# Model rows numbered in blocks of 128, the last token tile of each mixer turned and scored in column halves, its norm root on GpSimd, and fewer unread transposes

## What is computed

```python
for i in range(DEPTH):
    hn = rms_norm(h, norm_mix[i])
    h = h + (mla_mixer if i % 2 == 0 else gla_mixer)(hn, ...)
    h = h + hier_moe(rms_norm(h, norm_ffn[i]), ...)
return h[:, N_META:N_META + S]

def rms_norm(x, g):
    return x * rsqrt(mean(x * x, axis=-1) + EPS) * g

def hier_moe(t, ...):                       # 32 experts, D_EXPERT = 256
    g_logits = t @ w_rg + b_rg              # 4 groups: argmax
    e_logits = t @ w_re + b_re              # 8 experts of that group: top 2
    for e in range(N_EXPERTS):
        hid = silu(t @ w_gate[e]) * (t @ w_up[e])
        out = out + gates[:, e:e + 1] * (hid @ w_down[e])
```

## Time and profile before

| | us |
|---|---|
| median of 3 runs | 722.73 (720.85 to 727.63) |
| profiled execution, its time | 727.45 |
| span of that execution | 725.7 |
| PE busy | 653.9 (90%) |
| DVE busy | 245.9 (34%) |
| ACT busy | 149.1 (21%) |
| POOL busy | 41.2 (6%) |

### The profile page before, as it was taken

The page is one execution under the profiler, slowest core; times in us unless marked ns, Lnnn a source line. Parts: engine busy times, 40 slices in busy tenths (PEclk is TensorE's granted clock), DMA queues, the critical chain, the costliest instruction groups (busy, mean ns, idle before and its releaser), DMA issues.

```text
span 725.7 us, 11565 instructions
## 1 busy us (share of the span) xinstructions
PE 653.9 (90%) x5148; PEld 389.1 (54%) x5148; DVE 245.9 (34%) x522; ACT 149.1 (21%) x293; POOL 41.2 (6%) x62
## 2 busy tenths in 40 slices
PE   7999899999999977999789999989999996687686
PEld 6654775467456535635358644564665552434332
DVE  2136874154332331333053811321533331123112
ACT  2135663631001100000023412123310110000000
POOL 2033110000000000000020600010000000000000
PEclk9999999999999997999999999999999998899899
DMA  8910553737999999999993505644879999999995
GB/s 349 379 53 1 231 234 145 320 144 305 428 438 428 429 426 428 432 429 424 431 431 163 202 29 233 261 203 186 336 315 433 433 429 431 414 440 430 420 425 238
DMA packets 12311, 234.09 MB, mean 323 GB/s; under 512 B 1552, under 2 KB 1872, under 8 KB 3168
## 3 DMA queue, kind: packets, MB, share of 16 engines
q1 hardware_dynamic: 11936, 233.09, 76.5%
q10 hardware_dynamic: 320, 0.18, 0.1%
HBM read 232.22 MB, written 1.05 MB: 321 GB/s over the span
## 4 chain that ended last, share of the span: by engine, by line
PE 69%; DMA 25%; issue 2%; DVE 2%; ACT 1%; SPq 0%; DVEq 0%; ACTq 0%
DMA mem<-in_experts 23%; PE ps L945 10%; PE ps L1112 8%; PE ps L670 7%; PE ps L967 7%; PE ps L921 7%; PE ps L959 5%; PE ps L790 4%; PE ps L1103 4%; PE ps L742 3%; PE ps L732 1%; DMA mem<-in_mla_w_in 1%; PE ps L715 1%; PE ps L810 1%; PE ps L686 1%
## 5 line engine op out<-in xcount | busy, mean ns | idle before, releaser
L945 PE MATMUL ps<-mem,hT 128*32 128x256 f32 x1952 | 120.3, 393 | 25.7 <-DMA mem<-in_experts 25.6
L945 PEld LDWEIGHTS ps<-mem,hT 128*32 128x32 f32 x1952 | 65.0, 113 | 81.5 <-DMA mem<-in_experts 33.1
L921 PE MATMUL ps<-mem,rows 128*128 128x128 f32 x560 | 71.4, 290 | 16.1 <-issue 16.1
L921 PEld LDWEIGHTS ps<-mem,rows 128*128 128x128 f32 x560 | 68.7, 204 | 22.1 <-issue 22.1
L967 PE MATMUL ps<-hT,mem 128*128 128x512 f32 x160 | 76.4, 609 | 2.1 <-DVE hT L1788 1.8
L1794 DVE TENSOR_TENSOR rows<-rows,ps 128x512 f32<-128x512 f32 (+1 forms) x80 | 54.2, 684 | 59.2 <-PE ps L967 59.1
L959 PE MATMUL ps<-mem 128*32 128x512 f32 x496 | 59.1, 606 | 7.7 <-DMA mem<-in_experts 5.4
L670 PE MATMUL ps<-mem,hT 128*128 128x512 f32 x128 | 57.1, 598 | 2.9 <-ACT hT L1428 2.9
L1112 PE MATMUL ps<-mem,hT 128*128 128x512 f32 x128 | 55.6, 594 | 0.0
L1348 ACT ACTIVATE mem<-ps 128x256 f32<-128x256 f32 x16 | 9.9, 620 | 218.2 <-PE ps L945 218.2
L967 PEld LDWEIGHTS ps<-hT,mem 128*128 128x128 f32 x160 | 24.0, 170 | 49.5 <-issue 49.5
(11 more groups left out here) (303 smaller groups left out, 674.5 us busy)
## 6 DMA issues: line engine op xcount, KB each, us to landing
mem<-in_experts SPq DMA_DIRECT2D x34, 4096.0 KB, 31.9
mem<-in_experts SPq DMA_DIRECT2D x24, 2048.0 KB, 17.4
mem<-in_gla_parts SPq DMA_DIRECT2D x4, 4096.0 KB, 25.4
rows<-in_experts SPq DMA_DIRECT2D x4, 2048.0 KB, 34.4
mem<-in_mla_o SPq DMA_DIRECT2D x1, 4096.0 KB, 30.3
mem<-in_mla_w_in SPq DMA_DIRECT2D x2, 1344.0 KB, 10.2
mem<-in_mla_uq SPq DMA_DIRECT2D x1, 2304.0 KB, 16.9
mem<-in_mla_ukv SPq DMA_DIRECT2D x1, 2048.0 KB, 23.5
```

Of the source, the lines that this page charges most:

```text
L921: mm = pe.matmul(ps[:, k // 4, (k % 4) * P:(k % 4 + 1) * P], xn[:, i, k, :], Sg[:, i, :], start=i == 0, stop=i == nt - 1)
L945: mm = pe.matmul(ps[32 * j:32 * j + 32, 2, m * FE:(m + 1) * FE], xe[:, k, 32 * j:32 * j + 32], w[:, j, c * FE:(c + 1) * FE], start=k == 0 ...
```

## The change

The numbering of model rows changes from stride 8 to blocks of 128 (piece k holds rows 128k to 128k+127), in the kernel's views and in the host's layout of all weights. With it a half of the columns of a tile holds four whole pieces, and tile 1 is turned, multiplied by its gain, and scored in two halves; its first half is turned ahead of `ranks(early)`, right behind the last product. The scores stand ahead of all of `gathered(early)`. On DVE `gained(n, 1)` moves ahead of `ranked` and `sent`. The squares of the expert norms stay on ACT (those of tile 1 in two halves, each after its add), the roots go to GpSimd. `BUSY` goes from 24 and 36 to 6 and 14, `FILL` is gone. ACT gets an `Exp` of one element behind `scaled(1)`.

```diff
-    FILL, BUSY = [3, 5], [24, 36]
+    BUSY = [6, 14]
+    HALVED = (1, 3)
+    HT0 = [sum(NORM_TILES[:i]) + sum(m < i for m in HALVED) for i in range(5)]
 # gpsimd, ahead of its wait for moe_done, and again at its end with n = 3
+        def roots(n):
+            for i in ORDER[n]:
+                pool.wait_ge(ffn_squared, rstd_count(n, i))
+                v = ssq[:, i:i + 1]
+                link(pool.tensor_scalar(v, v, ssq_right if i == 1 else 0.0, EPS, ALU.add, ALU.add))
+                pool.tensor_tensor(rstd[:, i:i + 1], v, half_root[:, i:i + 1], ALU.pow).then_inc(rstd_ok, 1)
 # tensor
-        def turn(i, src):
-            for k in range(KD):
+        def turn(i, ks=range(KD)):
+            for k in ks:
...
-                mm = pe.transpose(dst, src[0:R, k, :], ident[0:R, 0:R])
+                mm = pe.transpose(dst, h[i][0:R, k * P:(k + 1) * P], ident[0:R, 0:R])
...
             early = ORDER[n][:-1]
+            turn(1, range(HK))
             pe.wait_ge(sel_ok, 3 * l + 1)
             ranks(early, 4)
             pe.wait_ge(*H_DONE[n][1])
-            turn(1, h[1].rearrange("p (q k) -> p k q", k=KD))
+            turn(1, range(HK, KD))
+            for b in range(2):
+                pe.wait_ge(hT_ok, HT0[n] + NORM_TILES[n] + b)
+                logits_by_token(l, 1, range(HK * b, HK * (b + 1)))
             pe.wait_ge(*xn_ready(n, 0))
             pe.wait_ge(sel_ok, 3 * l + 2)
-            gathered(early, range(FILL[l]), True)
-            pe.wait_ge(hT_ok, NB[n] + NORM_TILES[n])
-            logits_by_token(l, 1)
-            gathered(early, range(FILL[l], KD), True)
+            gathered(early, range(KD), True)
             for _ in range(BUSY[l]):
                 pe.transpose(ps[:, 4, 0:P], ident, ident)
 # scalar
-        def scale_of(n, i):
-            link(square(n, i))
-            v = ssq[:, i:i + 1]
-            link(act.activation(v, v, ACT.Ln, bias=eps_b))
-            return act.activation(rstd[:, i:i + 1], v, ACT.Exp, scale=-0.5)
-
         def scaled(i):
-            act.activation(xn[:, i], h[i].rearrange("p (q k) -> p k q", k=KD), ACT.Copy,
+            act.activation(xn[:, i], h[i].rearrange("p (k q) -> p k q", k=KD), ACT.Copy,
                            scale=rstd[:, i:i + 1]).then_inc(xn_act, 1)
...
+            for i in ORDER[n][:-1]:
+                square(n, i).then_inc(ffn_squared, 1)
             for i in ORDER[n]:
                 if i == 1:
                     act.wait_ge(lg_done, l + 1)
                     act.copy(lgT[0:NG + NE, c0:COL[1]], ps[0:NG + NE, 5, 0:COL[1] - c0]).then_inc(lg_copied, 1)
-                scale_of(n, i).then_inc(rstd_ok, 1)
+                    for b, done in ((0, HALF_ADDED[l]), (1, H_DONE[n][1])):
+                        act.wait_ge(*done)
+                        ins = act.activation(xflat[:, D + 512 * b:D + 512 * (b + 1)], h[1][:, 512 * b:512 * (b + 1)], ACT.Square,
+                                             scale=D ** -0.5, accum_out=(ssq[:, 1:2], ssq_right)[b])
+                    ins.then_inc(ffn_squared, 1)
                 act.wait_ge(rstd_ok, rstd_count(n, i))
                 if i != 1:
                     scaled(i)
             scaled(1)
+            act.activation(fix[0:1, 1:2], one_b[0:1], ACT.Exp)
 # vector, gained(n, i) for n in HALVED and i == 1: a wait and a signal for each half
+                    if halved:
+                        dve.wait_ge(xn_turned, HT0[n] + ORDER[n].index(i) + 1 + b)
                     ins = TT(hT[:, 4 * b:4 * b + 4, cols], ps[:, 2 * i + b, :].rearrange("p (k q) -> p k q", k=4),
                              rep(gn[:, n, 4 * b:4 * b + 4], P), ALU.mult)
+                    if halved and b == 0:
+                        ins.then_inc(hT_ok, 1)
 # vector, mixer_added
+            gained(n, 1)
             ranked(l, EARLY_TILES[l], 1, 4)
             sent(EARLY_TILES[l], slice(0, GE)).then_inc(sel_ok, 1)
-            gained(n, 1)
             route_last(l)
```

More of the change, by code:

```diff
@@ L29 @@
 KD = D // P
+HK = KD // 2
 SEQ, META = 256, 16
@@ L344, in build @@
     NORM_TILES = [3, 3, 3, 2]
-    NB = [sum(NORM_TILES[:i]) for i in range(5)]
     ORDER = [[0, 1, 2], [2, 0, 1], [0, 1, 2], [0, 1]]
@@ L472, in _ @@
             sp.dma_start(wz[:, HK * wz_:HK * (wz_ + 1), :],
-                         a["mla_w_in"][0].rearrange("(p k) n -> p k n", k=KD)[:, HK * wz_:HK * (wz_ + 1), :]).then_inc(done, 16)
+                         a["mla_w_in"].rearrange("p (k n) -> p k n", k=KD)[:, HK * wz_:HK * (wz_ + 1), :]).then_inc(done, 16)
         sp.dma_start(cst[:, P:BW], a["const"][:, P:BW]).then_inc(in_c, 16)
@@ L639, in norm @@
                 pe.wait_ge(*H_DONE[n][i])
[L640 to L643 removed]
+                turn(i)
+        def turn(i, ks=range(KD)):
+            for k in ks:
                 R = WID[i]
                 dst = ps[:, 2 * i + k // 4, (k % 4) * P:(k % 4 + 1) * P] if i < 2 else ps[:, 4, k * R:(k + 1) * R]
[L646 removed]
+                mm = pe.transpose(dst, h[i][0:R, k * P:(k + 1) * P], ident[0:R, 0:R])
             mm.then_inc(xn_turned, 1)
@@ L660, in mixer_out @@
                                 pe.wait_ge(*H_DONE[n][t])
-                                turn(t, h[t].rearrange("p (q k) -> p k q", k=KD))
+                                turn(t)
                         if (i, b, k) == (1, 0, 6):
-                            pe.wait_ge(hT_ok, NB[n] + NORM_TILES[n] - 1)
+                            pe.wait_ge(hT_ok, HT0[n] + NORM_TILES[n] - 1)
                             pe.wait_ge(in_moe, IN_MOE)
@@ L693, in logits_turned, with logits_by_token @@
             mm.then_inc(lg_turned, 1)
-        def logits_by_token(l, i):
-            for k in range(KD):
+        def logits_by_token(l, i, ks):
+            for k in ks:
                 mm = pe.matmul(ps[:, 6, (NG + NE) * i:(NG + NE) * (i + 1)], hT[:, k, COL[i]:COL[i] + P], wr[:, l, k, :],
                                start=k == 0, stop=k == KD - 1)
-            mm.then_inc(lg_turned, 1)
+            if KD - 1 in ks:
+                mm.then_inc(lg_turned, 1)
         def ranks(tiles, bank, ahead=()):
@@ L1450, in gained @@
         def gained(n, i):
-            dve.wait_ge(xn_turned, NB[n] + ORDER[n].index(i) + 1)
             cols = slice(COL[i], COL[i] + WID[i])
+            halved = n in HALVED and i == 1
+            if not halved:
+                dve.wait_ge(xn_turned, HT0[n] + ORDER[n].index(i) + 1)
             if i < 2:
                 for b in range(2):
+                    if halved:
+                        dve.wait_ge(xn_turned, HT0[n] + ORDER[n].index(i) + 1 + b)
                     ins = TT(hT[:, 4 * b:4 * b + 4, cols], ps[:, 2 * i + b, :].rearrange("p (k q) -> p k q", k=4),
                              rep(gn[:, n, 4 * b:4 * b + 4], P), ALU.mult)
+                    if halved and b == 0:
+                        ins.then_inc(hT_ok, 1)
             else:
@@ L1917, in _ @@
         moe(1)
-NAMES = ["x", "meta_tokens", "mla_w_in"]
+NAMES = ["x", "meta_tokens"]
 def laid_out(inputs):
     x = {n: np.asarray(v) for n, v in inputs.items()}
-    def by_row(w, k):
-        return w.reshape(P, k * w.shape[1])
     def by_block(w, k=KD):
@@ L1936, in pad, with parts @@
         return full
-    def parts(w, k):
-        w = w.reshape(2, GROUPS, GE, P, 2, k // 2 * w.shape[3])
-        return w.transpose(0, 1, 3, 4, 2, 5).reshape(2, GROUPS, P, -1)
+    def parts(w):
+        w = w.reshape(2, GROUPS, GE, 2, HK, P, w.shape[3])
+        return w.transpose(0, 1, 5, 3, 2, 4, 6).reshape(2, GROUPS, P, -1)
     def halves(w):
@@ L1946, in laid_out @@
     out = {}
-    out["experts"] = np.stack([parts(x["moe_w_gate"], KD), parts(x["moe_w_up"], KD), halves(x["moe_w_down"])], 2)
+    out["experts"] = np.stack([parts(x["moe_w_gate"]), parts(x["moe_w_up"]), halves(x["moe_w_down"])], 2)
     w = x["gla_w_in"][0]
     vo, ro = 2 * GH * GDK, 2 * GH * GDK + GH * GDV + GRANK
-    out["gla_parts"] = np.stack([by_row(w[:, 0:vo], KD), by_row(w[:, vo:ro - GRANK], KD), by_row(w[:, ro:], KD),
+    out["gla_parts"] = np.stack([by_block(w[:, 0:vo]), by_block(w[:, vo:ro - GRANK]), by_block(w[:, ro:]),
                                  by_block(x["gla_w_o"][0])])
     out["mla_o"] = by_block(x["mla_w_o"][0])
+    out["mla_w_in"] = by_block(x["mla_w_in"][0])
     out["gains"] = np.stack([x["norm_mix"][0], x["norm_ffn"][0], x["norm_mix"][1], x["norm_ffn"][1]])\
-        .reshape(4, P, KD).transpose(1, 0, 2)
+        .reshape(4, KD, P).transpose(2, 0, 1)
     both = np.concatenate([x["mla_g_qn"][0], x["mla_g_kn"][0]])
@@ L1965, in laid_out @@
         out["gate_up"][QUAD * j:QUAD * j + GRANK] = x["gla_w_gate_up"][0]
-    out["late"] = np.concatenate([router[0], router[1], np.tile(bias, (P, 1)), by_row(low, KD),
+    out["late"] = np.concatenate([by_block(router[0]), by_block(router[1]), np.tile(bias, (P, 1)), by_block(low),
                                   x["gla_b_gate"][0].reshape(GH, P).T, x["gla_g_out"][0].reshape(GDV // P, P).T], 1)
```

12 lines of the change are left out of this document (7 added, 5 removed).

## The result

The changed kernel takes 719.03 us (median of 14 runs, 714.92 to 724.60), the kernel before 723.77 (14 runs, 720.74 to 727.63). The ratio is 0.9931, with a 95% interval of 0.9908 to 0.9955: 5.0 us less, between 3.3 and 6.7. Forecast were 5.2 us less.

A forecast was written before the change was run, and what follows sets the result against it. The prediction took DMA to bound the expert phases and PE's chain the stretches between; 2.2 (layer 0) + 2.6 (layer 1) + 0.4 (contiguous transposes) = 5.2 us off the 722.7 median gave 717.5 us, range 713.0 to 722.0.

The forecast's parts named there:

- What bounds: Expert phases: DMA-bound, 376 us in all; an earlier first read brings SyncE's issue and the phase's end forward one for one.
- up to some 3 us: Ahead of each layer's expert phase: the gain that can pass to its end while the DMA queue is empty.
- Halves: Tile 1 before the expert phase: turning and scoring it in halves brings layer 0's scores 1.9 us earlier.
- PE's queue in layer 0: Gathers and fillers behind the scores: PE binds by 0.7 us, and tile 1's ranks start 2.2 us earlier.
- Layer 1: Ahead of layer 1's expert phase: the choice binds, and tile 1's ranks start 2.6 us earlier.
- Roots: Expert norms: moving the roots to GpSimd costs nothing, with 0.55 us of cover in layer 1 and 0.7 more in layer 0.
- The rival with the late root: GpSimd takes twice as long or locks with DVE: root 0.8 us late, 0.9 us lost, 718.4 us; chance 0.12.
- Contiguous transposes: Output products of both layers and layer 1's opening norm: contiguous rows load faster, 0.4 us in all.
- The clock: Rival: fewer fillers let PE's clock halve ahead of the expert phases, costing 7.6 us, to 725.1; chance 0.04.
- a rule by which taking fillers away can't lower it: PE's clock: by the Trainium skill transposes don't count as activity, so the fillers never held it up.
- Sum: Whole kernel: 2.2 + 2.6 + 0.4 = 5.2 us less.

The follow-up runs named there:

- no_fillers: The changed kernel without any unread transpose ahead of the expert phases; ratio to the kernel before 0.9924 (0.9901 to 0.9947).
- whole_turn: The changed kernel with tile 1 turned, multiplied and scored whole instead of in halves; ratio to the kernel before 1.0059 (1.0035 to 1.0082).
- sent_first: The changed kernel with `ranked` and `sent` of the early tiles ahead of tile 1's gain on VectorE; one run, 724.15 us.
- roots_act: The changed kernel with the roots of the expert norms back on ScalarE, by Ln and Exp; ratio to the kernel before 0.9948 (0.9919 to 0.9977).
- one_choice: The changed kernel with tile 1's second expert choice left out altogether (results wrong), 0 and 8 unread transposes; ratio to the kernel before 0.9912 (0.9878 to 0.9945).
- whole_filled: The changed kernel with tile 1 turned and scored whole, plus 12 unread transposes between turning and scores; ratio to the kernel before 0.9976 (0.9945 to 1.0008).
- root_late: The changed kernel with one more power of four columns on GpSimd ahead of tile 1's root; one run, 715.12 us.
- fillers_cut: The kernel before with only its unread transposes cut from 24 and 36 to 6 and 14; ratio to the kernel before 1.0001 (0.9978 to 1.0023).
- gather_between: The changed kernel with three (layer 0) and five (layer 1) rounds of the early gathers ahead of the scores again; one run, 726.86 us.
- short_choice: The changed kernel with three instructions of tile 1's second choice moved behind its signal, 0 and 8 unread transposes; ratio to the kernel before 0.9894 (0.9848 to 0.9939).

## Why the prediction was right, point by point

- **What bounds.** Right. Seam and stream are independent. In all fourteen profiled executions, with seams of layer 0 from 11.8 to 17.6 us, the product behind layer 0's last wait for weights starts 185.4 to 186.1 us after the issue. In layer 1 it is 185.8 to 186.1 in ten; in the other four (`no_fillers`, `whole_turn`, `sent_first`, `roots_act`) the last product comes 1.1 to 1.8 us later, behind one at a low clock (3.55 us for 1.9 in `sent_first`). That is the clock of the last group; DMA is as busy up to it as in the others. The "up to some 3 us" that can pass were 3.4 in layer 1 (from 528.50, when DMA falls idle, to 531.87), of which the change used 2.62 and `one_choice` the rest.
- **Halves.** Right. Scores end 2.63 us after the add's end for 2.68 worked out; undone (`whole_filled`) they cost 1.9 us in each layer, the 1.9 of the sum.
- **PE's queue in layer 0.** Term of the sum 2.2, measured 2.57. PE binds as forecast, by 0.4 us instead of 0.7. The gathers start at 156.33, 0.2 us ahead of the modelled end of the scores, and the fillers follow 3.57 us later, not 3.70: I had laid modelled ends of groups one behind the other that overlap by a few tenths.
- **Layer 1.** Term 2.6, measured 2.62, bound by the choice.
- **Roots.** Free, as forecast. The power of one column takes 0.56 us, not 1.04 as with four, so the cover is 0.75 us where I had 0.55. The rival with the late root didn't come; `roots_act` shows what the step is for. Nor did VectorE and GpSimd lock each other out: `sent` (155.50, 0.42 us, as long as before) starts inside the power (155.14 to 155.70), and in layer 1 of `root_late` a `sent` of 0.29 us, as long as in the changed kernel, lies inside a power of 1.02 us.
- **Contiguous transposes.** Term 0.4. Measured 0.45 in layer 0's product, 0.06 at the opening norm (1.10 to 1.04 us for its first eight), nothing in layer 1's product (0.87 in both). The sixteen in layer 0's output product gave 0.45 where I had 0.2: I had the saving from eight of 128 rows and applied it to eight of the 16-row tile as well, where it is larger.
- **The clock.** The changed kernel keeps 1.00 through both seams, so the rival didn't come, and the pauses that I had worked out (0.65 and 0.4 us) were indeed harmless. But the reasoning around them fell. I took the long idle time of the earlier trace rows for the only kind that lowers the clock, and weighed a rule by which taking fillers away can't lower it. `fillers_cut`, `no_fillers`, `whole_turn` and `gather_between` lower it behind idle times of 1.38 to 1.88 us, and the twelve transposes of `whole_filled` hold it up. In the changed kernel the longest idle time at the seams is 0.73 us; its 14 fillers of layer 1 (1.56 us) cover most of the 1.88 us for which PE stands idle in `no_fillers`. The trace of the kernel before already held a sign that I had passed over: at the end of layer 0's experts, behind a wait of 0.98 us that follows other waits, the product takes 3.23 us for 1.96 at a clock of 0.50. Timeline of PE and stretch (columns as above):

```profile
356.71 3.23 PE L959 MATMUL ps<-mem 128*32 128x512 f32 x16 [0.98 <-DMA mem<-in_experts]
```

```profile
358.00:359.00 1.00, 1.00 (x12) 0.20 (x4) 0.00 (x0) 0.00 (x0) 0.00 (x0) 0.50 1.26 541
```

  The chance of 0.04 was too small for a kernel that trims just these instructions.
- **Sum.** 5.2 us forecast; 2.57 + 2.62 + 0.5 = 5.7 in the traces, 5.0 in the timed runs. Counted from layer 0's last product, layer 1's issue came 2.46 us earlier (175.16 and 172.70), where I had 2.8: of the 0.2 us that contiguous transposes were to give in between they gave 0.06, and the product at a low clock behind the last weights took 0.24 us more (3.47 for 3.23). That 5.0 stands so close to 5.2 says little, as its interval is 3.4 us wide; the terms rest on the seams.

## What to carry to other kernels

Where a stream of weights bounds a phase and its queue runs empty ahead of it, work on the time from the last input to the first read: it passes one for one until the queue no longer runs empty, and can be read to 0.1 us in a single trace where the total time can't be. Work that looks like surplus in such a place has two prices, the time by which it is late and the idle time that it covers; cut it to just under the next wait, and look at the granted clock of every experiment before its time. Moving an instruction behind a signal gains nothing if the next consumer's producer is queued behind it on the same engine.

## What the runs showed of the hardware

- **Short pauses lower the clock, sometimes.** In the seams of these kernels no idle time of PE up to 0.93 us was followed by a lower clock. Of nine between 1.30 and 1.88 us, six were (1.38 twice, 1.46 twice, 1.47, 1.88), and three were not (1.30, 1.45 in `short_choice`, 1.67 in `roots_act`). The price was 1.3 to 2.0 us of the seam in four of them, and 3.3 and 2.7 in `whole_turn`, where the clock stayed at 0.50 for 6 us or more. In the expert phases, where PE has waited for weights several times just before, even shorter ones are: each of the fourteen traces has a wait of 0.95 to 1.09 us ahead of a product near the end of either layer, and 9 of these 28 products took 2.97 to 3.6 us for 1.9. The length of one pause alone, then, doesn't tell whether the clock falls. The same kernels dip elsewhere too, at places that change from one execution to the next, which is part of why a total time says less than a seam.
- **Transposes hold the clock.** Twelve transposes of an identity in a pause of 1.38 us kept the granted clock at 1.00 (`whole_filled` against `whole_turn`), and 36 of them alone, 3.96 us in layer 1 of the kernel before, left it there from 523 to 527 us. By the Trainium skill (TensorE: Matmul & The Clock Gate, Part 4), the full clock does not engage for transpose mode, which does not count as PE being busy in the same way; here transposes kept it, and the measurement decides. That the prediction took it to mean not at all was more than the page says. Whether transposes alone would raise a lowered clock no run here shows.
- **Strided reads on ScalarE.** With 32 bytes from one float32 to the next, the copy of 128x1024 takes 2.16 us, contiguous 1.15.
